# A decoder step on one Trainium2 core: the second layer's dilated projections as seven block products, with tokens normalized as they are turned

## The reference, cut to what matters

```python
DILATED = ((128, 1), (512, 4), (2048, 16))
kv = (rmsnorm(x, g_kv) @ w_kv).reshape(b, t, N_DIL, 2, N_KV_B, HEAD_DIM)
k = rmsnorm(kv[:, :, :, 0], k_norm[:, None, :])            # then rope
q = rmsnorm((rmsnorm(x, g_attn[1]) @ w_q).reshape(b, t, N_DIL, N_HEADS_B, HEAD_DIM), q_norm[:, None, :])  # then rope
for g, (window, dil) in enumerate(DILATED):                # attention of each group
    o, lse = local_attend(q[g], k[g], v[g], window mask)   # groups combined with softmax(lse)
xp = xp + combined @ w_o
```

## Time and profile before

| | us |
|---|---|
| median of three runs | 1359.59 |
| the profiled execution, its own time | 1362.34 |
| its span, first to last instruction | 1360.5 |
| PE busy in the span | 1275.2 (94%) |
| DVE busy | 639.7 (47%) |
| POOL busy | 495.3 (36%) |
| ACT busy | 331.5 (24%) |
| layer 2 up to the end of its main loop, in the span | 582.3 to 1049.7 |

### The profile page before, as it was taken

The page is one execution under the profiler, slowest core; times in us unless marked ns, Lnnn a source line. Parts: engine busy times, 40 slices in busy tenths (PEclk is TensorE's granted clock), DMA queues, the critical chain, the costliest instruction groups (busy, mean ns, idle before and its releaser), DMA issues. The chain is left out here.

```text
span 1360.5 us, 20795 instructions
## 1 busy us (share of the span) xinstructions
PE 1275.2 (94%) x8580; PEld 894.0 (66%) x8580; DVE 639.7 (47%) x1018; ACT 331.5 (24%) x667; POOL 495.3 (36%) x415
## 2 busy tenths in 40 slices
PE   8999999999999988899999999999998999997786
PEld 6787887546566654458877877877755666664443
DVE  3578775524522211173559559558436572221114
ACT  2223322302122222140115015015005312222112
POOL 4466744101111111016876576576450111111101
PEclk8999999999999999899999999999999989999899
DMA  8446635577799999961113012013050899999996
GB/s 310 140 141 220 220 122 197 189 309 279 315 417 418 418 418 420 376 244 59 52 56 97 9 55 97 9 56 97 9 140 6 344 357 418 418 419 419 419 419 265
DMA packets 92768, 318.82 MB, mean 234 GB/s; under 512 B 32969, under 2 KB 45401, under 8 KB 66564
## 3 DMA queue, kind: packets, MB, share of 16 engines
q1 hardware_dynamic: 77956, 279.95, 52.9%
q0 software_dynamic: 13536, 33.29, 6.9%
q10 hardware_dynamic: 1184, 4.26, 0.8%
HBM read 300.19 MB, written 33.28 MB: 245 GB/s over the span
## 5 line engine op out<-in xcount | busy, mean ns | idle before, releaser
L2069 PE MATMUL ps<-slots 128*128 128x384 f32 x768 | 262.0, 495 | 1.1 <-DVE vo L2368 0.7
L2069 PEld LDWEIGHTS ps<-slots 128*128 128x128 f32 x768 | 203.0, 270 | 43.9 <-issue 3.2
L1215 PE MATMUL ps<-slots,oT 128*64 128x256 f32 x1216 | 160.9, 398 | 23.5 <-DMA slots<-in_w_up 21.9
L1215 PEld LDWEIGHTS ps<-slots,oT 128*64 128x64 f32 x1216 | 108.4, 144 | 72.6 <-issue 24.9
L1241 DVE TENSOR_TENSOR sg<-sg,ps 64x256 f32<-64x256 f32 x64 | 26.4, 413 | 242.9 <-ACT sg L1238 242.9
L1727 POOL DMA_INDIRECT xs<-xn_rows,idx x30 | 30.7, 1024 | 238.8 <-PE ps L1204 166.5
L1733 POOL DMA_INDIRECT y_rows<-ysb,idx x30 | 30.1, 1005 | 172.4 <-DVE ysb L1250 172.4
L1238 ACT ACTIVATE sg<-ps 64x256 f32<-64x256 f32 x64 | 24.4, 381 | 237.1 <-PE ps L1215 237.1
L1250 DVE COPY ysb<-ps 64x512 f32<-64x512 f32 x60 | 41.6, 694 | 85.8 <-PE ps L1233 79.9
L602 PE MATMUL ps<-xnT_a,wA 128*128 128x260 f32 (+1 forms) x320 | 76.9, 397 | 1.5 <-DVE xnT_a L866 1.4
L1233 PE MATMUL ps<-slots,hT 128*64 128x512 f32 x320 | 74.0, 598 | 4.2 <-issue 4.2
(11 more groups left out here) (338 smaller groups left out, 2335.5 us busy)
## 6 DMA issues: line engine op xcount, KB each, us to landing
slots<-in_w_up SPq DMA_DIRECT2D x42, 1024.0 KB, 28.0
slots<-in_w_down SPq DMA_DIRECT2D x40, 1024.0 KB, 29.0
slots<-in_w_gate SPq DMA_DIRECT2D x34, 1024.0 KB, 25.9
slots<-in_unit_weights_b SPq DMA_DIRECT2D x12, 1536.0 KB, 6.8
wA<-in_qkv_pairs_a SPq DMA_DIRECT2D x24, 512.0 KB, 3.8
apart<-in_w_gate SPq DMA_DIRECT2D x10, 1024.0 KB, 28.0
spare<-in_w_gate SPq DMA_DIRECT2D x8, 1024.0 KB, 27.8
scratch<-in_w_gate SPq DMA_DIRECT2D x8, 1024.0 KB, 28.5
```

Of the source, the lines that this page charges most:

```text
L1215: last = nc.tensor.matmul(bank(q)[lo:lo + CAP, 0:FE], x[:, k, :], wt[:, k, :], start=(k == 0), stop=(k == KT - 1))
L2069: last = nc.tensor.matmul(bank(i % 2)[:, 0:UW], xT[:, kt, cols], wB[:, g, kt, :], start=(kt == 0), stop=(kt == KT - 1))
```

## The change

1. **Seven of the twelve units** (n = 2, 4, 5, 7, 8, 10, 11: `mixed(n)`) are projected by a two by two block scheme with seven products in place of eight. Tokens are halved into chunks 0, 1 and 2, 3, K into 4 and 4 tiles, columns into 192 and 192. Each product (a **part**) is 8 matmuls, 16 records: four K tiles for each of two token chunks, 192 columns streamed. Parts 0 to 6 are `mixed_part`'s (the order in which `ahead` calls them is `PARTS`). Part 7 is the decoding tokens as before. PE's waits for DVE stay as they were, now from part to part.
2. **Block sums.** DVE forms four sums of tokens once (`mix_tokens`, 1024 elements a partition each) and four sums of weights for each of the seven units (`mix_weights`, 768 elements each, two SBUF operands). The products are added up partly in PSUM, partly by DVE in `evict_mixed`.
3. **Gapless copies.** ACT copies the token blocks that these products use unmixed to contiguous places, once. Unit 11's part 2 still reads `xT` with the step of four, as its copy's place is needed by then.
4. **Tokens normalized at their turn.** `turn_x` becomes a matmul with a diagonal of 1/rms: x is squared first, POOL makes 1/rms, ACT makes the diagonal, and only then PE turns. Evictions are plain copies, and the trip of 1/rms through DRAM is gone.
5. **Gains by ACT.** All units but (0, 1) have their weights scaled by ACT, 16 instructions a unit, after `turned(j, 0)` and `turned(j, 1)`.
6. In the passes j = 0 to 2, `ahead(1, 4)` and part 0 of unit (j+1, 1) move ahead of group 2's turns, part 1 behind them.

```diff
-            NSTEP, NPART, NCHUNK = sum(STEPS), 8, NT
-            UQ = UW // 4
+            NSTEP, NPART = sum(STEPS), 8
+            UQ, UH, HK = UW // 4, UW // 2, KT // 2
+            PARTS = ((0, 1), (2, 3), (4, 5), (6,), (7,))
+
+            def mixed(n):
+                return n > 1 and n % NDIL > 0
+
+            chunk0, mixed0 = [0], [0]
+            for n in range(NDIL * NKV):
+                chunk0.append(chunk0[-1] + (8 if mixed(n) else NT))
+                mixed0.append(mixed0[-1] + (4 if mixed(n) else 0))
...
+                def mix_of(buf, k=HK):
+                    return buf.rearrange("p (k n) -> p k n", k=k)
+
+                t1, t2 = mix_of(grow[:, 0:HK * UH]), mix_of(grow[:, HK * UH:2 * HK * UH])
+                t3 = mix_of(slots[:, WB + NDIL * KT * UW:WB + NDIL * KT * UW + HK * UH])
+                copies = [flat(oT)[:, (NPAIR - 2 - 2 * i) * TOK:(NPAIR - 2 - 2 * i) * TOK + D].rearrange("p (k c m) -> p k c m", k=HK, c=2) for i in range(2)]
+                copy_01 = grow[:, 2 * HK * UH:2 * HK * UH + 512].rearrange("p (k c m) -> p k c m", k=2, c=2)
+                s_copy = sem("b_tokens_copied")
+                diag = grow[:, 0:2 * 128].rearrange("p (i n) -> p i n", i=2)
+                mix_x = [flat(apart)[:, D * i:D * i + D].rearrange("p (k c m) -> p k c m", k=HK, c=2) for i in range(4)]
+                x_res = xT[:, :, 0:SEQ].rearrange("p k (i r) -> p k r i", r=4)
...
-                    sp.wait_ge(norm.s_rstd, NT)
-                    sp.dma_start(rs_rows.rearrange("(t p) -> p t", p=128), rs[:, 0:4], allow_slow_non_contiguous=True).then_inc(s_rso, 16)
-                    sp.wait_ge(s_rso, 16)
-                    sp.dma_start(rsr[:, :], rs_rows.rearrange("(i r) -> i r", r=4)).then_inc(s_rsi, 16)
...
-                        pe.wait_ge(s_cb, 3 * t + 3)
+                        pe.wait_ge(s_dg, t + 1)
                         dst = bank(TURN_BANK[t], 2).rearrange("p (k m) -> p k m", k=KT)
                         for kt in range(KT):
-                            last = nc.tensor.transpose(dst[:, kt, 0:rows], x[0:rows, t, kt:D:KT], ident[0:rows, 0:rows])
+                            last = nc.tensor.matmul(dst[:, kt, 0:rows], x[0:rows, t, kt:D:KT], diag[0:rows, t % 2, 0:rows], start=True, stop=True)
                         last.then_inc(s_xt, 1)
...
+                        if mixed(n):
+                            for part in PARTS[c]:
+                                mixed_part(n, part)
+                            return
...
+                    def mixed_part(n, part):
+                        g, i, w = n % NDIL, chunk0[n] + part, wB[:, n % NDIL]
+                        lower = copies[1] if n < NDIL * NKV - 1 else x_res[:, HK:KT, 0:2]
+                        if part == 0:
+                            pe.wait_ge(s_ws, 2 * n + 2)
+                            pe.wait_ge(s_mix, 4)
+                            pe.wait_ge(s_copy, 5)
+                        elif part in (1, 3, 5):
+                            pe.wait_ge(s_wm, mixed0[n] + (2, 3, 4)[part // 2])
+                        pe.wait_ge(s_ev, i - 1)
+                        if part == 7:
+                            last = sample_rows(i, g)
+                        else:
+                            tokens = (copies[0], mix_x[1], lower, mix_x[2], mix_x[0], None, mix_x[3])[part]
+                            for c in range(2):
+                                for k in range(HK):
+                                    cols = (w[:, k, 0:UH], t2[:, k], w[:, HK + k, 0:UH], t3[:, k], t1[:, k],
+                                            t2[:, k], w[:, HK + k, UH:UW])[part]
+                                    if part == 5:
+                                        rows = copy_01[:, k, c, :] if k < 2 else (copy_2, copy_3)[k - 2][:, 128 * c:128 * c + 128]
+                                    else:
+                                        rows = tokens[:, k, c, :]
+                                    last = nc.tensor.matmul(bank(i % 2)[:, UH * c:UH * c + UH], rows, cols,
+                                                            start=(part in (0, 1, 4) and c == 0 and k == 0), stop=(part in (2, 5, 6) and c == 1 and k == HK - 1),
+                                                            skip_group_check=True)
                         last.then_inc(s_proj, 1)
...
+                        if more:
+                            ahead(1, 4)
+                            parts(0)
...
                         turn_back(j, 2, 2)
-                        ahead(1, 4)
+                        if not more:
+                            ahead(1, 4)
+                        parts(1)
                         scores(j, 2, 0)
                         ahead(2, 0)
+                        parts(2)
                         scores(j, 2, 1)
                         ahead(2, 1)
+                        parts(3, 4)
 
...
                         turn_p(j, 2)
                         weigh(j, 1)
-                        ahead(2, 3)
+                        parts(6)
                         turn_p(j, 3)
                         weigh(j, 2)
                         turn_p(j, 4)
                         weigh(j, 3)
-                        ahead(2, 4)
+                        parts(7)
...
+                    def scale(g, i, ks):
+
+                        lo, hi = ((0, 2 * HD), (2 * HD, UW))[i]
+                        for k in ks:
+                            last = nc.scalar.activation(wB[:, g, k, lo:hi], wB[:, g, k, lo:hi], ACT.Copy, scale=gcol[:, i, k:k + 1])
+                        return last
+
+                    def scale_unit(j, g):
+
+                        act.wait_ge(s_unit[g], 16 * j + 16)
+                        for i in range(2):
+                            scale(g, i, range(KT)).then_inc(s_ws, 1)
+
+                    scale(0, 0, range(KT)).then_inc(s_ws, 1)
+                    scale(0, 1, range(KT - 3))
                     for t, rows in TILES:
+                        act.wait_ge(s_cb, 3 * t + 3)
+                        norm.square(act, t, junk)
+                        if t == 0:
+                            scale(0, 1, range(KT - 3, KT)).then_inc(s_ws, 1)
+                        act.wait_ge(norm.s_rstd, t + 1)
+                        nc.scalar.activation(diag[0:rows, t % 2, 0:rows], ident[0:rows, 0:rows], ACT.Copy, scale=rs[0:rows, t:t + 1]).then_inc(s_dg, 1)
                         act.wait_ge(s_xt, t + 1)
                         src = bank(TURN_BANK[t], 2).rearrange("p (k m) -> p k m", k=KT)
                         nc.scalar.activation(xT[:, :, 128 * t:128 * t + rows], src[:, :, 0:rows], ACT.Copy).then_inc(s_xc, 1)
-                        norm.square(act, t, junk)
+                    act.wait_ge(s_ws, 4)
+                    scale_unit(0, 2)
+                    act.wait_ge(s_xc, 4)
+                    nc.scalar.activation(copies[0], x_res[:, 0:HK, 0:2], ACT.Copy).then_inc(s_copy, 1)
+                    nc.scalar.activation(copies[1], x_res[:, HK:KT, 0:2], ACT.Copy).then_inc(s_copy, 1)
+                    nc.scalar.activation(copy_01, x_res[:, HK:HK + 2, 2:4], ACT.Copy).then_inc(s_copy, 1)
+                    for k, dst in ((2, copy_2), (3, copy_3)):
+                        nc.scalar.activation(dst.rearrange("p (c m) -> p c m", c=2), x_res[:, HK + k, 2:4], ACT.Copy).then_inc(s_copy, 1)
 
...
+                        turned(j, 0)
+                        if j < NKV - 1:
+                            scale_unit(j + 1, 0)
+                            scale_unit(j + 1, 1)
+                        turned(j, 1)
+                        if j < NKV - 1:
+                            scale_unit(j + 1, 2)
+                        turned(j, 2)
...
+                    def evict_mixed(j, g, part):
+
+                        i = chunk0[3 * j + g] + part
+                        got = bank(i % 2)[:, 0:UW].rearrange("p (c n) -> p c n", c=2)
+                        first_p = tok[:, g, 2:4, 0:UH]
+                        early, late = tok[:, g, 0:2, UH:UW], tok[:, g, 2:4, UH:UW]
+                        dve.wait_ge(s_proj, i + 1)
+                        if part == 0:
+                            room(j, g)
+                            V.tensor_copy(first_p, got).then_inc(s_ev, 1)
+                        elif part in (1, 3):
+                            dve.wait_ge(s_ev, i)
+                            V.tensor_tensor(early if part == 1 else late, first_p, got, ALU.add).then_inc(s_ev, 1)
+                        elif part == 2:
+                            V.tensor_copy(tok[:, g, 0:2, HD:UH], got[:, :, HD:])
+                            V.tensor_copy(vo[:, j % 2, g, 0:2, :], got[:, :, 0:HD]).then_inc(s_ev, 1)
+                        elif part in (4, 6):
+                            dve.wait_ge(s_ev, i)
+                            half = late if part == 4 else early
+                            V.tensor_tensor(half, half, got, ALU.add).then_inc(s_ev, 1)
+                        elif part == 5:
+                            dve.wait_ge(s_ev, i)
```

(49 more changed lines are left out.)

109 lines of the change are left out of this document (61 added, 48 removed).

## The result

The changed kernel takes **1382.82 us** (median of 4 runs, 1380.88 to 1383.57) where the kernel before takes 1358.61 (4 runs, 1355.29 to 1359.62) beside it: ratio 1.018, 95% interval 1.0158 to 1.0202, so 24.2 us slower. Forecast were 1353.3 us, 1346 to 1361, and faster.

A forecast was written before the change was run, and what follows sets the result against it. PE's matmul stream bounds the main loop, with a DVE chain in each pass's second half. Start +6.5, three passes -10.8, last pass -2.0 sum to -6.3 us: 1359.59 becomes 1353.3, range 1346 to 1361.

The forecast's parts named there:

- the seven products: Projections: a part takes 2.61 us, saving 3.2 a unit, 22.4 for seven, were PE alone the bound.
- the 1.2 that I had taken: Unit 11's part 2, which keeps strided loads: extra cost between 0 and 2.3 us, middle taken.
- the forecast -2.0: Last pass: 3.2 us saved less 1.2, as DVE sums nothing there and PE doesn't wait.
- The upper end: Unit 11's part 2: highest price of its strided loads, 2.3 us, 1 us later than the sum.
- the fourth scores: First half of a pass: PE waits 1.3 us for DVE's masking, so 1.8 of 3.1 us is saved.
- DVE's chain: Second half of a pass: DVE works without a gap and sets the end; 1.8 of 3.3 us saved.
- rival A: Whole kernel: PE stays the bound and DVE's block sums fit; 14.7 us saved, 1344.9; chance 0.12.
- the joined maxima take 0.65: Second half of a pass: DVE's step before ACT's exponentials takes 0.65 us; PE then waits 1.0.
- Rival C: In the passes, DVE's block sums wait for POOL's instructions: 5.8 us more a pass, 1370.7; chance 0.12.
- 0.9 more for each of five tiles: Start: a turn has 16 records instead of 8, costing 4.5 us in all.
- My bound of 10 for the start: Start: upper bound of the loss, 10 us against 6.5 forecast, if longer idle time brings back the low clock.
- D: Seven products: weight loads aren't hidden, a record costs 0.190 us, 21 us lost, 1374; chance 0.03.

The follow-up runs named there:

- the start repaired: Changed kernel with ACT writing the normalized rows and PE turning these by plain transposes: 1369.55 us, ratio 1.01 to the kernel before.
- both repairs: Changed kernel with POOL's long products held until the joined maxima are out, and ACT-scaled rows turned by plain transposes: 1350.85 us, ratio 0.9959.

## Why the prediction was wrong

- **Right: the seven products themselves.** Parts start 2.60 to 2.71 us apart, loads on the copies last 190 ns. Part 2 of unit 11 cost 3.79 instead of 2.6, the 1.2 that I had taken, and the last pass brought -1.9 of the forecast -2.0. For the strided load, rule and trace agree in kind (Trainium skill, "SBUF — State Buffer", section "Door 1: The DMA port swizzle"): 330 ns against 190. The upper end, which the rule put nearer, was too high.
- **Right, once the meeting is gone: a pass.** In the first half PE waited 0.86 to 1.14 us before the fourth scores, forecast 1.3. With the meeting gone a pass takes 98.70 us, forecast 98.6; the second half, from `ahead(1, 4)` on, takes 46.3, forecast 46.0, with DVE busy from the first copied turn to its end without a gap: the reading of DVE's chain held. One reading beneath it was wrong. The prediction has PE standing still at two places before the change; there are four (also 0.75 and 0.17, at 842.41 and 844.70), and the 0.75 is a meeting with POOL inside the chain. So the chain could be shortened: moving that addition and the last copy took 2.9 us off each pass, to the 96 that rival A had named. ACT's scaling was hidden, as costed.
- **Wrong, the larger part of the wrong sign: "the joined maxima take 0.65".** This step kept the duration of before and did not ask where POOL's front would be beside it. I had noted that `ahead(1, 4)` and part 0 were put before group 2's turns, and used it only as room for POOL. It moved the start of the front from 5.4 to 10.5 us ahead of the last scores, and so the two long products onto the maxima: 6.1 us instead of 0.65, and up to 2.9 more of low clock on PE. Forecast -10.8 for three passes, measured +8.1; the run with POOL held gives 20.2 back, 18.2 of them in the traces' three passes.
- **Rival C had the mechanism and the wrong place.** I looked for it at the added instructions, the block sums. Most of them met nothing (0.95 to 0.96 us). One in each pass, for part 5, took 4.32 beside POOL's products, past the 1.2 that I had named as C's sign, and cost nothing: it ended at 773.67 and part 5 came at 779.21, as the prediction had argued. What cost was the old, tiny instructions on the critical chain. C's threshold, 2.1 us a pass, was passed: against the forecast the passes lost 18.9 us in all, 6.3 each, and C had priced 17.4. I also took it that only instructions with two SBUF operands wait. L2567 has one and waited 3.41. The rule that I had cited (Trainium skill, "SBUF — State Buffer", section "Who interferes with whom") names tensor_scalar too, in its two-port modes; the trace agrees as far as the instruction goes (which mode it ran in is not shown), and I had read only half of the rule.
- **Wrong: "0.9 more for each of five tiles".** The second eight records of a turn were priced at the pace of the transposes (8 in 0.9), whose loads take 192 ns, though the product loads x with a step of eight. It costs 2.8 to 3.0 more for each, 14.3, not 4.5. The row that warns of it stood in rows 5: 308 ns for strided loads. I had used it for unit 11 and not here. The run with gapless loads gives the 0.11 a record that I had assumed. The first turn came 2.1 later (forecast 2.7), 2.6 went to the low clock behind the last tile's turn, and 1.1 came back where the wait of 0.73 had stood: 17.9 in all. My bound of 10 for the start knew a low clock, but not this turn.
- **The range** ended at 1361 and left out C and D, at 1370.7 and 1374 the rivals in the direction of the result. D, loads that aren't hidden, did not happen in the seven products, but in the turns. Each failed step alone would have left it: with POOL held the time is 1362.59, with the start repaired 1369.55.

## What to carry to other kernels

When a change moves work in program order, list what the other engine does beside each short instruction on the critical chain, before and after. Here the moved start of a long GpSimd instruction mattered more than the added instructions, and one wait that holds it back was worth more (20 us) than the change itself (5.5 with both repairs). A price is taken from a row with the same number of records and the same duration of its weight loads. And removing one meeting can move the other engine's work onto the next: look at what stands there first.

## What the runs showed of the hardware

- An f32 product (two records) whose stationary operand has a step of eight elements runs at 0.23 us a record with 128 columns, with a step of four at 0.24 with 192; gapless 0.111 and 0.163. Transposes that address x with the same step of eight took 0.11 a record, one record each, with loads of 192 ns.
- POOL's power of 25 elements, 4.36 us long, does not hold DVE up: in the changed kernel a block sum at 826.83 ran beside the one of 825.80 in 0.96. Its products of 1600 elements held up the DVE instructions with two SBUF operands that began beside them, and L2567 with one, until they had ended.
- The meeting costs both sides: POOL's own instructions (six tree additions, one product) grew from 4.82 to 6.64 and from 3.31 to 4.67 beside DVE's mixes of 2.0 us.
- After PE had stood still for 5.8 us its clock was at the lower level for about 5 us in pass j = 1 (PEclk 0.50 from 839.30 to 845, 0.77 over the stretch shown), and filling the gap with unread products brought 5.7 us in the kernel's time. In the same place with rows scaled on ACT the idle time was the same, and part 5 was slowed by only 0.5 us, so the length of the slow stretch is not fixed.
